# Nine modulation units loaded at once at the start, rotary tables later, first weight splits ahead of the norms at layer seams, and layer loops written out

## The reference

```
mod = silu(c) @ w_ada[l] + b_ada[l]              # six vectors of 1024: sh1 sc1 g1 sh2 sc2 g2
h = rmsnorm(x, norm1_w) * (1 + sc1) + sh1
u = h @ w_in                                     # 1024 x 5632: pool, conv, q, k, v, gates
q, k = rope(rmsnorm(q)), rope(rmsnorm(k))        # tables: cos and sin of position * frequency
merged = gates0*(pool @ p_pool) + gates1*(conv @ p_conv) + gates2*(attention @ p_attn)
x = x + g1 * (merged @ w_out)
h2 = rmsnorm(x, norm2_w) * (1 + sc2) + sh2
x = x + g2 * ((silu(h2 @ w_gate) * (h2 @ w_up)) @ w_down)
```

## Time and profile before

| | |
|---|---|
| median of 3 runs | 1988.18 us (1981.52 to 1988.48) |
| profiled execution, its own time | 1982.71 us |
| its span in the trace | 1981.0 us |
| mean granted clock of TensorE | 0.919 of full speed |
| busy, share of the span | PE 1639.4 us (83%), DVE 968.2 (49%), ACT 618.2 (31%) |
| HBM read | 425.30 MB |
| first product starts | 67.45 us |
| second layer of the first block, first product | 562.43 us |
| second block, first product of its two layers | 1039.60 and 1511.57 us |

### The profile page before, as it was taken

The page is one execution under the profiler, slowest core; times in us unless marked ns, Lnnn a source line. Parts: engine busy times, 40 slices in busy tenths (PEclk is TensorE's granted clock), DMA queues, the critical chain, the costliest instruction groups (busy, mean ns, idle before and its releaser), DMA issues.

```text
span 1981.0 us, 21880 instructions
## 1 busy us (share of the span) xinstructions
PE 1639.4 (83%) x7670; PEld 1135.3 (57%) x7670; DVE 968.2 (49%) x1418; ACT 618.2 (31%) x872; POOL 29.2 (1%) x59
## 2 busy tenths in 40 slices
PE   1789786999778978799969685999986887699995
PEld 1568675777556866677848564433334766433331
DVE  6785576644478557664455674111105575411112
ACT  1335524333233552433323460111113453111111
POOL 2000000000000000000020000000000000000000
PEclk9989997999978999899989787999997988699998
DMA  8774355745478335354545306799994313599995
GB/s 310 250 269 139 112 180 200 258 128 191 151 245 286 128 124 175 120 188 138 179 129 179 108 1 255 283 387 387 387 387 146 124 42 116 202 386 387 387 387 195
DMA packets 199069, 427.97 MB, mean 216 GB/s; under 512 B 8065, under 2 KB 16449, under 8 KB 198945
## 3 DMA queue, kind: packets, MB, share of 16 engines
q1 hardware_dynamic: 195328, 417.43, 60.0%
q0 software_dynamic: 3360, 8.87, 1.6%
q10 hardware_dynamic: 256, 0.08, 0.0%
HBM read 425.30 MB, written 1.05 MB: 215 GB/s over the span
## 4 chain that ended last, share of the span: by engine, by line
PE 36%; SPq 12%; DVE 6%; issue 4%; DMA 2%; ACT 2%; DVEq 0%; POOL 0%; ACTq 0%
SPq L663 12%; PE gp L1853 10%; PE gp L2015 8%; PE gp L2176 7%; PE gp L2161 2%; DMA raw_deep<-in_exp_w_down 1%; PE mp L2207 1%; PE mp L2073 1%; PE mp L2083 1%; PE mp L2084 1%; PE mp L2034 1%; PE mp L2092 1%; DVE acc L1077 0%; PE mp L2105 0%; PE mp L2104 0%
## 5 line engine op out<-in xcount | busy, mean ns | idle before, releaser
L1143 DVE TENSOR_TENSOR wlo<-raw,whi 128x2048 fp32r<-128x2048 f32 (+1 forms) x132 | 289.7, 2194 | 280.3 <-ACT whi L764 278.0
L1853 PE MATMUL gp<-whi,xt_hi 128*128 128x512 f32 (+1 forms) x800 | 321.1, 401 | 60.8 <-DVE xt_lo L1187 31.4
L764 ACT ACTIVATE whi<-raw 128x2048 fp32r<-128x2048 f32 (+1 forms) x132 | 241.9, 1835 | 391.7 <-PE gp L1853 281.8
L1853 PE MATMUL gp<-wlo,xt_hi 128*128 128x512 f32 (+1 forms) x800 | 313.7, 392 | 0.0
L1853 PE MATMUL gp<-whi,xt_lo 128*128 128x512 f32 (+1 forms) x800 | 313.6, 392 | 0.0
L1853 PEld LDWEIGHTS gp<-whi,xt_hi 128*128 128x128 f32 x800 | 156.4, 196 | 103.8 <-issue 42.0
L1853 PEld LDWEIGHTS gp<-whi,xt_lo 128*128 128x128 f32 x800 | 155.9, 195 | 31.6
L1853 PEld LDWEIGHTS gp<-wlo,xt_hi 128*128 128x128 f32 x800 | 156.4, 196 | 29.8 <-issue 0.5
L1721 DVE TENSOR_SCALAR pr<-slots,key,dg 128x128 f32<-128x128 f32 x64 | 19.3, 345 | 260.0 <-PE gp L2197 260.0
L1077 DVE SCALAR_TENSOR_TENSOR acc<-raw,cact,acc 128x1024 f32<-128x1024 f32 x99 | 127.0, 1283 | 10.7 <-DMA raw<-in_w_ada 8.6
L2015 PE MATMUL gp<-whi,xt_hi 128*128 128x512 f32 (+1 forms) x224 | 85.4, 381 | 7.6 <-DVE xt_lo L1501 7.6
(11 more groups left out here) (374 smaller groups left out, 2438.1 us busy)
## 6 DMA issues: line engine op xcount, KB each, us to landing
raw<-in_w_in SPq DMA_DIRECT2D x60, 1024.0 KB, 5.5
raw<-in_w_ada SPq DMA_DIRECT2D x48, 1024.0 KB, 5.4
raw_deep<-in_exp_w_down SPq DMA_DIRECT2D x36, 1024.0 KB, 14.1
raw_deep<-in_exp_w_gate SPq DMA_DIRECT2D x30, 1024.0 KB, 14.1
raw_deep<-in_exp_w_up SPq DMA_DIRECT2D x30, 1024.0 KB, 14.2
raw<-in_w_gate SPq DMA_DIRECT2D x20, 1024.0 KB, 5.1
raw<-in_w_up SPq DMA_DIRECT2D x20, 1024.0 KB, 5.1
raw<-in_w_down SPq DMA_DIRECT2D x20, 1024.0 KB, 4.9
```

The costliest lines, as they stand in the source:

```text
L764: act.activation(slot(whi, s % SPLIT, units, cols), slot(raw, g % RAW, units, cols), ACT.Copy).then_inc(hi_done.sem, 1)
L1143: dve.tensor_tensor(slot(wlo, s % SPLIT, units, cols), slot(raw, g % RAW, units, cols), slot(whi, s % SPLIT, units, cols).bitcast(F32), AL ...
L1853: mm = pe.matmul(gp[:, q % 2, t, 0:wide], a[:, chunk, ts], w[:, unit, c0:c0 + wide], start=first and n == 0 and m == 0, stop=last and n == ...
```

## The change

Seven edits, in one change:

1. SP loads the identity, c alone (`crows`), unit 0, `x` and units 1 to 7 with no wait between them, the first three to `raw` and the rest to `raw_deep`; then the first two `w_in` units, unit 8, and the constant tables. ACT's split 0 waits until units 0 to 7 are read, since its target lies on `raw_deep`.
2. DVE's angles come behind split 2 of layer 0 and its cosine and sine copies behind split 5 (`angles()`, `rope()`, the same instructions as before).
3. DVE's first row norm stands between the units; PE turns the normed x before the two modulation sums and not after them.
4. `LATE` = 2: each `ada` unit of the table goes two splits later, and two fewer splits with a unit stand before the first product. In the last layer the nine units of a layer that does not exist are no longer multiplied or summed; `sum_mod(5)` moves from product `S_FF` + 3 to `S_FF` + 5.
5. The splits 0 and 1 of a next layer (split 0 of the second block too) stand before the norm, and the first two modulation vectors of layer 1 are taken during the down products of layer 0.
6. POOL loads the `lnw` rows of the second block's first norm once `acc`, on whose memory they now lie, is summed for the last time.
7. All layer loops are Python loops, so that each layer has code of its own with constants in its waits; the copies `pcur`, `qkcur`, `poolcur` are gone.

```
-AFTER = {s: AHEAD + s for s in range(12)}
-AFTER.update({S_FF + i: AHEAD + 12 + i for i in range(6 * ADA - 1 - 12)})
+LATE = 2
+AFTER = {LATE + s: AHEAD + s for s in range(12)}
+AFTER.update({S_FF + LATE + i: AHEAD + 12 + i for i in range(6 * ADA - 1 - 12)})
 AFTER[S_DOWN + 6] = 6 * ADA + AHEAD - 1
...
         @block.sync
         def _(sp):
-            for name, tile in (("c_ident", ident[:, :]), ("c_mask", mask[:, :]),
-                               ("c_count", count[:, :, :].rearrange("p a t -> p (a t)")), ("c_freq", freq[:, :]),
-                               ("c_order", order[:, :, :].rearrange("p a n -> p (a n)")),
-                               ("c_lam", lamc[:, :, :].rearrange("p l n -> p (l n)"))):
-                sp.dma_start(tile, A[name]).then_inc(consts_in, 16)
+            sp.dma_start(ident[:, :], A["c_ident"]).then_inc(ident_in, 16)
+            sp.dma_start(crows[:, :], A["c"][0].rearrange("(a p) -> a p", p=P)).then_inc(c_in, 16)
+            def load_early(n):
+                src, units, cols = weights(("ada", n), 0)
+                sp.dma_start(early(n), src.rearrange("(k p) n -> p k n", p=P)).then_inc(early_in[n], 16)
+            load_early(0)
+            sp.dma_start(x[:, :, :], A["x"].rearrange("b (t p) d -> p (b t) d", p=P)).then_inc(x_in, 16)
+            for n in range(1, 2 * ADA):
+                load_early(n)
...
-            for n in range(AHEAD):
-                if n >= RAW:
-                    sp.wait_ge(*raw_read[n % RAW].at(0, (n - AHEAD) // RAW))
-                load_group(("ada", n), 0, n)
-                if n == 0:
-                    sp.dma_start(x[:, :, :], A["x"].rearrange("b (t p) d -> p (b t) d", p=P)).then_inc(x_in, 16)
-            with sp.Fori(0, LAYERS) as l:
+            for g, item in enumerate(RING1[0:2]):
+                sp.wait_ge(*raw_read[g % RAW].at(0, g // RAW))
+                load_group(item, 0, g)
+            load_early(2 * ADA)
+            for name, tile in (("c_freq", freq[:, :]), ("c_mask", mask[:, :]),
+                               ("c_count", count[:, :, :].rearrange("p a t -> p (a t)")),
+                               ("c_order", order[:, :, :].rearrange("p a n -> p (a n)")),
+                               ("c_lam", lamc[:, :, :].rearrange("p l n -> p (l n)"))):
+                sp.dma_start(tile, A[name]).then_inc(consts_in, 16)
+            for l in range(LAYERS):
                 for g, item in enumerate(RING1):
+                    if l == 0 and g < 2:
+                        continue
...
-                        with sp.If(l < LAYERS - 1):
+                        if l < LAYERS - 1:
                             load_group(item, l, g)
-                        with sp.Else():
+                        else:
                             sp.sem_inc(landed[g % RAW].sem, 16)
...
-            pool.wait_ge(*x_final.at(LAYERS, 0))
             def norm_rows(gain, bias):
                 pool.dma_start(lnw[:, 0, :], gain.partition_broadcast(P)).then_inc(lnw_in.sem, 16)
                 pool.dma_start(lnw[:, 1, :], bias.partition_broadcast(P)).then_inc(lnw_in.sem, 16)
+            pool.wait_ge(*acc_read.at(LAYERS - 1, 6))
             norm_rows(A["ln_in_g_2"], A["ln_in_b_2"])
+            pool.wait_ge(*x_final.at(LAYERS, 0))
...
-            act.wait_ge(ang_ready, 1)
-            act.activation(angk[:, :, :, :], ang[:, :, :, :], ACT.Sin).then_inc(rope_ready, 1)
-            act.wait_ge(params_ready, LAYERS)
-            act.activation(csig[:, :], pcol[:, 0, PC_LAYER:PC_ROWS], ACT.Sigmoid).then_inc(csig_ready, 1)
+            act.wait_ge(c_turned, 1)
+            act.activation(csig[:, :], mp[:, 2, 0:KD], ACT.Sigmoid).then_inc(csig_ready, 1)
...
                 act.wait_ge(*x_final.at(l, 0))
                 normalise(xn1, 0)
-                split(0)
-                split(1)
+                if l == 0:
+                    act.wait_ge(*acc_done.at(0, 2))
+                    split(0)
                 for b in range(4):
                     high(X_NORM1 + b, xt_hi[:, 2 * b:2 * b + 2, :])
+                if l == 0:
+                    split(1)
                 for s in range(10):
                     split(s + 2)
                     if s % 2:
                         take_w_in(s // 2)
+                    if l == 0 and s == 1:
+                        act.wait_ge(ang_ready, 1)
+                        act.activation(angk[:, :, :, :], ang[:, :, :, :], ACT.Sin).then_inc(rope_ready, 1)
                     if s == 5:
...
                     split(s + 2)
                     if s == S_DOWN + 1:
                         high_plain(2, X_ACT + 2 * (FF_BLOCKS - 1), at_hi[:, FF_CHUNKS - 2:FF_CHUNKS, :])
+                if l < LAYERS - 1:
+                    split(0, l + 1)
+                    split(1, l + 1)
...
-                split(0)
-                split(1)
+                if l == 0:
+                    split(0)
+                    split(1)
+                    layer_norm_root((rv2_ready.sem, 1))
...
+                if l < LAYERS - 1:
+                    for slot_read in deep_read:
+                        act.wait_ge(*slot_read.at2(l, TURNS))
+                    split(0, l + 1)
                 layer_norm_root(rv2_ready.at2(l, 4))
+                if l < LAYERS - 1:
+                    split(1, l + 1)
...
+                def early_ada(n):
+                    vec, i = divmod(n, ADA)
+                    dve.wait_ge(early_in[n], 16)
+                    if i == 0:
+                        dve.wait_ge(*acc_read.at(0, vec - 1))
+                    w, a = early(n), acc[:, vec % 2, :]
+                    for k in range(2):
+                        c = cact[:, 2 * i + k:2 * i + k + 1]
+                        if i == 0 and k == 0:
+                            ins = dve.tensor_scalar(a, w[:, k, :], c, None, ALU.mult)
+                        else:
+                            ins = dve.scalar_tensor_tensor(out=a, in0=w[:, k, :], scalar=c, in1=a, op0=ALU.mult, op1=ALU.add)
+                        if k == 0:
+                            lk(ins)
+                    ins.then_inc(early_read, 1)
+                    dve.wait_ge(early_read, n + 1)
+                    if n < RAW:
+                        dve.sem_inc(raw_read[n].sem, 1)
+                    if i == ADA - 1:
+                        dve.sem_inc(acc_done.sem, 1)
...
-                    if s in AFTER:
+                    if s in AFTER and l == LAYERS - 1 and AFTER[s] >= 6 * ADA:
+                        g = G_OF["ada", AFTER[s]]
+                        dve.wait_ge(*landed[g % RAW].at(l, 16 * (g // RAW + 1)))
+                        dve.sem_inc(raw_read[g % RAW].sem, 1)
+                    elif s in AFTER:
                         ada(AFTER[s], G_OF["ada", AFTER[s]], l, lk)
...
-                lk(dve.tensor_copy(pcur[:, :], pcol[:, bass.ds(l, 1), 0:PC_LAYER].rearrange("p a n -> p (a n)")))
-                lk(dve.tensor_copy(qkcur[:, :, :].rearrange("p a n -> p (a n)"), qkw[:, bass.ds(l, 1), :, :].rearrange("p a b n -> p (a b n)")))
-                lk(dve.tensor_copy(poolcur[:, :, :].rearrange("p a n -> p (a n)"), poolw[:, bass.ds(l, 1), :, :].rearrange("p a b n -> p (a b n)")))
-                row_norm(0)
-                take_mod(0)
-                take_mod(1)
-                norm_columns(0, 0)
-                split(0)
-                split(1)
+                if l == 0:
+                    dve.wait_ge(csig_ready, 1)
+                    lk(dve.tensor_tensor(cact[:, :], mp[:, 2, 0:KD], csig[:, :], ALU.mult))
+                    early_ada(0)
+                    early_ada(1)
+                    dve.wait_ge(params_t, LAYERS)
+                    for i in range(LAYERS):
+                        dve.tensor_copy(pcol[:, i, :], mp[:, i, 0:PC_ROWS]).then_inc(params_ready, 1)
+                    dve.wait_ge(params_ready, LAYERS)
+                    early_ada(2)
+                    row_norm(0)
+                    for n in range(3, 2 * ADA):
+                        early_ada(n)
+                    take_mod(0)
+                    take_mod(1)
+                    norm_columns(0, 0)
+                else:
+                    row_norm(0)
+                if l == 0:
+                    split(0)
                 spread(X_NORM1, 4, (xt_hi, xt_lo), 0, normed(0, 0))
+                if l == 0:
+                    split(1)
+                    early_ada(2 * ADA)
+                    dve.wait_ge(params_in, PARAMS)
+                qkcur, poolcur = qkw[:, l, :, :], poolw[:, l, :, :]
                 for s in range(10):
                     split(s + 2)
                     if s % 2:
                         take_w_in(s // 2)
+                    if l == 0 and s == 0:
+                        angles()
+                    if l == 0 and s == 3:
+                        rope()
...
+                    if s == S_DOWN + 5 and l < LAYERS - 1:
+                        take_mod(0, l + 1)
+                        take_mod(1, l + 1)
+                        norm_columns(0, 0, l + 1)
```

(34 more changed lines are left out.)

182 lines of the change are left out of this document (87 added, 95 removed).

## The result

Four runs of the changed kernel took 1939.0 to 1943.5 us, median 1940.1; the kernel before, on the same chip, 1988.0. The ratio is 0.9765, with a 95% interval of 0.9743 to 0.9788. The forecast was 1944, its range 1928 to 1962. The profiled execution took 1939.0 us (span 1937.2), 43.7 less than the one of before; the forecast's sum was 41.3. So between the two profiled executions the total is right to 2.4 us (by the medians the forecast lies 3.9 above). Its terms are not as good as that.

A forecast was written before the change was run, and what follows sets the result against it. No single engine was taken to bound the whole: PE is busiest at 83%, and experts run at their transfers' 387 GB/s. Terms summed to -41.3 from 1982.7, giving 1941.4; half of 5.5 on top gave 1944, range 1928 to 1962.

The forecast's parts named there:

- The start: Up to the first product: eight units in flight at once, first product at 47.4 us, 20.0 earlier (bounds 16.6 and 23.0).
- 350 GB/s: Transfer rate assumed at the start for 10.8 MB: 31 us from 2.3 us, so unit 7 lands at 33.3.
- `w_in` of layer 0: First products of layer 0: later splits and tables give back part of the 20.0, leaving 13.8 at product 10.
- The shift: Ahead of PE's q and k turn: a unit now stands behind split 12, before take_mod(3), +2.6 us in each layer.
- `w_out`: Output products before the first residual: two units are gone, -2.0 us in each layer.
- Layer 0's feed-forward part: Gate and up products of layer 0: the same eleven units two splits later, 0 us, with +3 as the bound.
- Layer 1's feed-forward part: Feed-forward of layer 1: missing units -3.0 us, their two missing sums in the down products -3.4 us.
- The seams: Between first-block layers -12.4 us, between the blocks -4.7, between the second block's layers -5.2.
- (B): Whole kernel gains more: register steps -4, faster start, absorbed tables, PE at full clock at first products; 1932 us, chance 0.13.
- (C): Code fetch: each layer's own code costs fetches on the path, making the kernel slower, up to 2142 us; chance 0.04.
- (D): At the start, many transfers in flight hold up unit 0 and c, so DVE ends last; 0.20 together with (A).
- (A): DVE becomes the bound of `w_in`, so the gain is only 26 us: 1959; chance 0.20 together with (D).

The follow-up runs named there:

- three-in-flight kernel: The changed kernel with at most three of the first units in flight, unit n issued once unit n-3 is summed: 1940.7 us, ratio 0.9778.
- gate-load kernel: The changed kernel with GpSimd's two broadcast loads of the gate bias held until the eight units are summed: 1934.4 us, ratio 0.9749.
- their experiment: The changed kernel with angles and rotary tables computed by DVE between units 0 and 1, not behind splits 2 and 5: 1932.8 us, ratio 0.9747.
- its experiment: The changed kernel with take_mod(3) between the subtraction of split 12 and the unit behind it: 1935.2 us, ratio 0.9746.
- the shift's undoing: The changed kernel with gate and up units, and sum and take of vector 5, two splits earlier again: 1940.1 us, ratio 0.9780.
- the one with the padding: The changed kernel with an unused 32-byte buffer ahead of those of the feed-forward stage: 1943.9 us, ratio 0.9799.
- the one with the seam undone: The changed kernel with splits 0 and 1 of layer 1 behind the row norm again: 1947.3 us, ratio 0.9802.
- the kernel with split 0 under PE's second sum: The changed kernel with split 0 on DVE ahead of take_mod(1) at the start: 1937.7 us in one execution.

## Why the forecast was right, and where not

**The start** is the step that was mis-sized: 15.8 instead of 20.0, outside its bound of 16.6, and the first product, at 51.6, outside the 44 to 51 that were to show it. "350 GB/s" was right, and so was the amount; up to 33.3 us the trace has:

```profile
DMA packets 3471, 10.87 MB, mean 350 GB/s; under 512 B 547, under 2 KB 764, under 8 KB 3471
```

Wrong was that unit 7 has landed when these bytes have moved. It landed at 37.1 us, when 12.3 MB had: part of what was issued behind it (the first `w_in` units, from 20.3 us on) moved before its last bytes did. That is 3.8 of the 4.3 us by which it is summed later. The step "DVE does the other units in 21 us from about 7 us and so keeps up" was wrong too, and has the other 0.5. It took for granted that units land evenly, but unit 1 came 11.5 us after unit 0, with `x` and GpSimd's 1.3 MB beside it. From 19.2 us on, seven units (17.8 us together), the row norm's small steps (1.5), the column copies and 1.0 of waiting make the 21.0 us to 40.2. So two paths end within 0.5 us of each other, and shortening one brings little: with GpSimd's load held back unit 7 lands 3.1 us earlier, and the product comes 1.6 earlier. The three-in-flight kernel shows that unit 1's lateness is not the number of transfers, the gate-load kernel that GpSimd's load has a part in it (0.7 us). How much `x` has was not tried.

**`w_in` of layer 0** gave back 6.6, forecast 6.2. The tables count 3.5 of it by their experiment; I had 2 (bounds 0 and 7.9). Product 10 came at 123.1 us, not at 118 to 119, by the miss of the start and these 0.4, with DVE's `wlo` as the releaser, as named. The longest wait for `wlo` was 2.6 us, so the sign of being wrong (over 3 us in several products in a row) did not come.

**The shift** cost 2.4 and 3.4, forecast 2.6 each, and its experiment takes 2.8 and 3.1 back in the stretch itself. The unit's place ahead of `take_mod(3)` is shown to be the cause. **`w_out`** (-2.0) is confirmed in layer 0 by the shift's undoing (+3.0 at product 30); in layer 1 that run can't tell it from the differences between executions.

**Layer 0's feed-forward part**, forecast 0, gave 3.6. What it belongs to stays open in the main. Eleven executions of ten kernels that are alike from product 30 to 42 took 81.8 to 87.5 us there, mean 84.9; the two with the old order 88.25 and 88.9. The windows (PEclk is third from the end) of the changed kernel, then of the one with the padding, of the one with the seam undone, and of the kernel before go with the granted clock:

```profile
304.00:389.00 85.00, 74.63 (x310) 60.04 (x311) 63.51 (x47) 31.66 (x23) 0.00 (x0) 0.94 0.79 275
```

```profile
304.00:386.00 82.00, 72.99 (x309) 58.76 (x310) 63.56 (x46) 31.40 (x23) 0.00 (x0) 0.96 0.81 283
```

```profile
304.00:392.00 88.00, 77.19 (x310) 61.82 (x311) 63.58 (x47) 31.63 (x22) 0.00 (x0) 0.90 0.75 266
```

```profile
312.00:401.00 89.00, 77.80 (x310) 62.23 (x311) 58.80 (x43) 31.63 (x23) 0.00 (x0) 0.89 0.71 241
```

So most of that gain is where the clock stood at its lower level (1.2 GHz) for some products. Product by product, two parts can be told apart. Product 30 itself took 8.15 and 8.36 us in the two kernels with the old order and 7.2 in all twelve executions with the change or most of it; its windows, before and after:

```profile
312.39:320.54 8.15, 8.15 (x25) 6.50 (x25) 6.87 (x7) 2.43 (x2) 0.00 (x0) 0.66 0.11 17
```

```profile
304.06:311.25 7.19, 7.19 (x24) 5.79 (x25) 5.87 (x6) 2.45 (x3) 0.00 (x0) 0.76 0.05 7
```

This 1.0 us is the change's, though neither the loops (8.36) nor the units' shift (7.21 with it undone) bring it. Products 34 and 38 took 8.0 and 8.3 us before, 6.9 and 7.1 in the changed kernel's profile, but 8.4 and 8.2 in that of the kernel with split 0 under PE's second sum, whose instructions are the same there: one profile can't say whose that part is. Two executions of the changed kernel gave 84.5 and 84.3 for the twelve products.

**Layer 1's feed-forward part**: -3.3 and -3.6 for the units and sums, forecast -3.0 and -3.4. (The rows of the forecast make 3.3 for the units: two groups of 26.06 less 24.43.) The further 1.4 lies between products 57 and 65 (40.8 us instead of 42.25), where the padded kernel, at 42.0, gives 1.2 of it to the address.

**The seams**: 12.6, 5.4 and 4.7 against 12.4, 4.7 and 5.2; the terms' causes are shown for the splits (5.0), the rows of the norm (3.8) and the branch of the second block (3.2). At the third seam itself, from the final x to the product, it is 5.4 us (3.7 instead of 9.1); the forecast's rows make 5.3, the branch's 3.15 and one split, and it wrote 5.2. What the sum left out, and only rival (B) named, is that PE without a wait keeps its full clock: there the first matmul takes 0.79 us before and 0.52 after, and 12 matmuls later the gain is 6.7 us instead of 4.7. Up to the end of the kernel the stretch behind this seam gains 1.2.

So the total was close in part by luck: -3.6 and -1.9 in the feed-forward parts and -1.2 in the rest, none of them forecast, stood against the 4.2 missing at the start. The address has a part in both layers; in layer 0 this profile hides it behind the 8.36 us product. Of the rivals, (C) is refuted, and so is the cause that (D) gives, a late unit 0 and c. What (D) feared came all the same, by way of unit 1: DVE ends last, by 0.5 us, and not the landing. (Its reckoning counted unit 7's own 2.6 us on DVE's side alone; by its numbers DVE had 6.4 us to spare and not 3.8.) (A)'s premise, that DVE sets the pace from the start through `w_in`, is true, but at the price that the sum had for `w_in`; (B)'s -4 for register steps did not come: with the loops written out and nothing else, the down products stayed at 5.62 us. What part register steps may have in the rest of that kernel's 6.6 us no run separates from the branches.

## What to carry to other kernels

Put small work that an engine owes sooner or later where that engine waits for a transfer, not behind the first work of the next one; and order an engine's queue by who waits for the result (an add of 0.2 us stood behind a unit of 2.6, and PE behind it). When many loads are in flight together, read the landing of the one that is waited for: the forecast's 10.9 MB had moved at 33.3 us, and the unit was not there until 37.1. When buffers are removed or added, look at the addresses of the operands that stay.

## What the hardware showed that I had not expected

- The same matmul in the rounded format (128x512) took 390 ns at the full clock with the stationary buffer at a multiple of 64 bytes and 396 to 397 with it 32 bytes off. Both `at_hi` and `bt_hi` show it.
- The first 1 MB unit was there at 7.7 us, the next at 19.2, although the DMA engines were busy all the time between (349 GB/s from 4 to 24 us). Unit 7 landed 3.8 us after as many bytes had moved as had been issued up to it.
- Executions of instructions that are the same in one stage of 85 us differ by 5.7 us there, with granted clocks of 0.90 to 0.96. A single profile of a change of 5 us can't be read by its span, only by its places.
